# Gate of the feed-forward part applied to the experts' rows and to the shared weights; modulation sums in pairs

## What is computed

```python
c_act = jax.nn.silu(c)
for l in range(DEPTH):                                   # DEPTH = 2
    mod = c_act @ w_mod[l] + b_mod[l]                    # 6 parts of 1024
    sh_m, sc_m, g_m, sh_f, sc_f, g_f = [m[:, None, :] for m in jnp.split(mod, 6, axis=-1)]
    h = rms_norm(x, norm_mix_g[l]) * (1.0 + sc_m) + sh_m
    x = x + g_m * mixer(h, ...)
    h = rms_norm(x, norm_ffn_g[l]) * (1.0 + sc_f) + sh_f
    x = x + g_f * moe_ffn(h, ...)
```

## Time and profile before

| | |
|---|---|
| median of 3 runs | 2122.92 us (2121.61 to 2122.98) |
| the profiled execution | 2122.44 us |
| its span, first to last instruction | 2120.3 us |
| TensorE busy | 2038.6 us |
| VectorE busy | 955.1 us |
| ScalarE busy | 400.2 us |
| GpSimd busy | 59.7 us |
| rate of the transfers while pairs run (page, part 2) | 397 to 412 GB/s in most slices |
| first half of branch 2 ends on TensorE, layer 0 | 197.2 us |
| output projection, layer 0 | 313.5 to 341.1 us |
| shared expert's second product, layer 0 | from 375.4 us |
| pairs of experts, layer 0 | 393.6 to 911.2 us |
| pairs of experts, layer 1 | 1271.7 to 1790.0 us |

### The profile page before, as it was taken

The page is one execution under the profiler, slowest core; times in us unless marked ns, Lnnn a source line. Parts: engine busy times, 40 slices in busy tenths (PEclk is TensorE's granted clock), DMA queues, the critical chain, the costliest instruction groups (busy, mean ns, idle before and its releaser), DMA issues. The chain is left out here.

```text
span 2120.3 us, 30214 instructions
## 1 busy us (share of the span) xinstructions
PE 2038.6 (96%) x11316; PEld 1214.5 (57%) x11316; DVE 955.1 (45%) x1926; ACT 400.2 (19%) x795; POOL 59.7 (3%) x143
## 2 busy tenths in 40 slices
PE   5999999899999999989999989999999997999998
PEld 3847884545445454466588644545545443475475
DVE  3897534333333333359864253433333333252252
ACT  2133211111111111123231011111111112131131
POOL 1000003000000000000000030000000000010000
PEclk9999999999999999999999999999999998998999
DMA  9654548799999999767455548999999997441621
GB/s 348 205 208 164 199 152 342 289 412 401 397 406 400 407 399 400 303 226 231 159 206 192 191 186 336 397 410 398 405 400 404 397 412 240 163 127 28 224 77 43
DMA packets 148133, 598.08 MB, mean 282 GB/s; under 512 B 13036, under 2 KB 17760, under 8 KB 96608
## 3 DMA queue, kind: packets, MB, share of 16 engines
q1 hardware_dynamic: 146656, 594.06, 72.7%
q0 software_dynamic: 1408, 3.10, 0.6%
HBM read 596.07 MB, written 1.05 MB: 282 GB/s over the span
## 5 line engine op out<-in xcount | busy, mean ns | idle before, releaser
L1236 PE MATMUL banks<-weight_ring,h_t 128*64 128x512 f32 x2112 | 464.7, 592 | 3.3 <-DVE h_t L1991 3.3
L1236 PEld LDWEIGHTS banks<-weight_ring,h_t 128*64 128x64 f32 x2112 | 154.8, 137 | 300.8 <-issue 299.0
L1224 PEld LDWEIGHTS banks<-z,sp_ 128*128 128x128 bf16 x3168 | 180.3, 99 | 58.7 <-issue 51.9
L2016 DVE SCALAR_TENSOR_TENSOR o_parts<-banks,slot_weight,o_parts 128x512 fp32r<-128x512 f32 x132 | 99.1, 751 | 245.0 <-ACT o_parts L1522 245.0
L1996 DVE TENSOR_TENSOR z<-banks,z 128x256 f32<-128x256 f32 x66 | 28.0, 425 | 386.5 <-ACT z L1509 386.5
L1224 PE MATMUL banks<-z,sp_ 128*128 128x128 bf16 x3168 | 191.6, 221 | 5.1 <-DVEq L1981 5.1
L930 PE MATMUL banks<-h_t,weight_ring 128*128 128x256 f32 x768 | 170.0, 379 | 0.0
L930 PEld LDWEIGHTS banks<-h_t,weight_ring 128*128 128x128 f32 x768 | 145.4, 190 | 20.0 <-DMA weight_ring<-in_w_in 0.2
L1522 ACT ACTIVATE o_parts<-banks,slot_weight 128x512 fp32r<-128x512 f32 x132 | 90.8, 688 | 278.2 <-PE banks L1261 278.2
L1274 PE MATMUL banks<-o_parts,slot_of 128*128 128x512 f32 x528 | 140.0, 406 | 0.9 <-DVE o_parts L2016 0.9
L2253 PE MATMUL banks<-weight_ring,h_t 128*128 128x512 f32 (+2 forms) x384 | 134.3, 509 | 1.3 <-DMA weight_ring<-in_w_in 1.3
(11 more groups left out here) (479 smaller groups left out, 2139.6 us busy)
## 6 DMA issues: line engine op xcount, KB each, us to landing
weight_ring<-in_w SPq DMA_DIRECT2D x264, 1024.0 KB, 9.8
weight_ring<-in_w_in SPq DMA_DIRECT2D x36, 2048.0 KB, 10.3
slots<-in_w SPq DMA_DIRECT2D x68, 1024.0 KB, 9.1
weight_ring<-in_w_mod SPq DMA_DIRECT2D x24, 2048.0 KB, 11.5
qk<-in_w SPq DMA_DIRECT2D x32, 1024.0 KB, 8.4
...
```

Of the source, the lines that this page charges most:

```text
L1224: mm = nc.tensor.matmul(x_banks[half][:, kk * P:(kk + 1) * P], xn_parts[:, t, c, half * KT // 2 + kk, :], pick_hot[:, i % PAIRS, t, :], st ...
L1236: mm = nc.tensor.matmul(h_bank[own, :], x_blk[:, i, k, own], w13(2 * i + b)[:, :, k, :], start=(k == 0), stop=(k == KT - 1), skip_group_ch ...
L2016: v.scalar_tensor_tensor(o_parts[:, 1, col], o_banks[h][:], own, o_parts[:, 0, col].bitcast(F32), ALU.mult, ALU.subtract).then_inc(o_ready, 1)
```

## The change

**Modulation.** Sums of column chunks are made in pairs: `cols` of chunk c takes the parts of c and c + 1 (the two halves of one part of the modulation) and sums each with 64 columns into its own half of the bank's partitions. VectorE then picks once, with `ident_half`, the sum of the identity's two halves, and `col4` needs no adding of halves. The places change too: in layer 0 the transposes of x now stand ahead of parts 0 to 3 (`first`); sum 6 leaves its place behind the value projections, and pair 6/7 stands between the two halves of the first branch that runs, branch 2 (`half`); pair 8/9 takes the place of sums 7 to 9; sum 12 goes, and pairs 12/13 and 14/15 stand where sums 13 and 14, 15 stood. On ScalarE the copies of parts 0 to 3 go behind the first norm. The row chunks keep their sums.

**Gate.** `gate` of the feed-forward part no longer multiplies the token banks. GpSimd multiplies the shared expert's second weights with it, in place, once they and the gate are there; SyncE loads them behind `wo` 1, no longer as the last of the ring's loads. `o_split` becomes: VectorE writes bank x slot weight x gate to `o_gated`, ScalarE copies that, rounded, to the first part, VectorE subtracts the two for the second. Behind the last pair, `last_add` adds its rows token tile by token tile (before: column half by column half), and VectorE adds the banks to x with one operation each. For that ScalarE copies the last pair's slot matrix once more.

**Rest.** TensorE, not SyncE, frees the eight banks at the start; SyncE issues c ahead of the positions and doesn't wait for GpSimd.

```diff
 MOD_STEPS = {
-    "start": [("part", 0), ("part", 1), ("sum", 0), ("part", 2), ("sum", 1), ("part", 3), ("sum", 2), ("sum", 3)],
-    "ka": [("sum", 4), ("sum", 5)], "va": [("sum", 6)], "aT": [("sum", 7), ("sum", 8), ("sum", 9)],
+    "first": [("part", 0), ("part", 1), ("cols", 0), ("part", 2), ("pad", 0), ("pad", 1), ("pad", 2), ("pad", 3),
+              ("part", 3), ("cols", 2)],
+    "ka": [("sum", 4), ("sum", 5)], "half": [("cols", 6)], "aT": [("cols", 8)],
...
+                            for half in range(2):
+                                own = slice(64 * half, 64 * half + 64)
+                                if c in DVE_CHUNKS:
+
+                                    pe.wait_ge(dve_parts.sem, dve_parts.at(l, c + half - DVE_CHUNKS[0] + 1))
+                                    share = K.ones[:, 0:64]
+                                else:
+
+                                    pe.wait_ge(B[l]["mod_part", c + half].free, B[l]["mod_part", c + half].consumed_at(l))
+                                    share = K.part_share[:].to_broadcast([P, 64])
+                                mm = nc.tensor.matmul(bank[own, :], share, mod_part[c + half], start=True, stop=True,
+                                                      skip_group_check=True)
...
+                pool.wait_ge(shared2_filled.sem, shared2_filled.at(l, 16))
+                pool.wait_ge(gate_ready.sem, gate_ready.at(l))
+                nc.gpsimd.tensor_tensor(slots2[:, 1], slots2[:, 1], broadcast(gate[:, 1, :], 1, 2), ALU.mult)
...
+                def last_add():
+
+                    for t in range(T):
+                        for h in range(2):
+                            if t == 0:
+                                pe.wait_ge(o_ready, nth(last_turn, 2 * second + h))
...
+                        mm.then_inc(y_done.sem, 1)
...
                     for h in range(2):
+                        dve.wait_ge(o_done, nth(it, 2 * i + h))
+                        v.scalar_tensor_tensor(o_gated[h], o_banks[h][:], own, gate[:, 1, h * CHUNK:(h + 1) * CHUNK], ALU.mult,
+                                               ALU.mult).then_inc(o_gated_ready, 1)
+                    for h in range(2):
                         col = slice(h * CHUNK, (h + 1) * CHUNK)
                         dve.wait_ge(o_first_ready, nth(it, 2 * i + h))
-                        v.scalar_tensor_tensor(o_parts[:, 1, col], o_banks[h][:], own, o_parts[:, 0, col].bitcast(F32), ALU.mult,
-                                               ALU.subtract).then_inc(o_ready, 1)
+                        v.tensor_tensor(o_parts[:, 1, col], o_gated[h], o_parts[:, 0, col].bitcast(F32), ALU.subtract)\
+                            .then_inc(o_ready, 1)
...
+                    dve.wait_ge(y_done.sem, y_done.at(l, t + 1))
                     for h in range(2):
                         col = slice(h * CHUNK, (h + 1) * CHUNK)
-                        v.tensor_tensor(y_tmp[:], y_bank[t][h][:], gate[:, 1, col], ALU.mult)\
+                        v.tensor_tensor(K.x[:, t, col], K.x[:, t, col], y_bank[t][h][:], ALU.add)\
                             .then_inc(B[l]["=moe_y", t, h].free, 1)
-                        dve.drain()
-                        v.tensor_tensor(K.x[:, t, col], K.x[:, t, col], y_tmp[:], ALU.add)
-                        dve.drain()
```

134 lines of the change are left out of this document (70 added, 64 removed).

## The result

| | before | after |
|---|---|---|
| median | 2121.29 us (10 runs, 2120.40 to 2124.16) | 2109.14 us (10 runs, 2105.93 to 2117.84) |
| the profiled execution | 2122.44 us, span 2120.3 | 2107.32 us, span 2105.6 |
| mean granted clock of TensorE in it (1.00 is 2.4 GHz) | 0.986 | 0.991 |

The changed kernel takes 0.9941 of the time (95% interval 0.9929 to 0.9953), 12.2 us less. The runs of the changed kernel spread over 12 us, those of before over 4. Each run comes with its mean granted clock, and after the change the two go together: 2105.93 us at 0.993, 2108.20 at 0.990, 2111.45 at 0.987, 2115.50 and 2117.84 at 0.985.

The account below looks back on a forecast made before the run. TensorE, busy for 96% of the span, was taken as the bound. Terms -1.36 - 1.00 - 1.08 - 3.06 - 0.83 = -7.33 us led from 2122.44 to 2115.1 profiled, 2115.5 forecast for the median, range 2111.5 to 2119.5.

Parts of the forecast that it names:

- A pair of sums: Paired column sums: halves run side by side, 1.03 us for a pair against 1.72 for two full sums.
- Between the layers: From layer 0 to layer 1: VectorE's shorter chain of additions lets TensorE start 3.06 us earlier.
- the block's end: From layer 1 to the second block: 0.83 us less, with SyncE's loads last instead of VectorE.
- The sentence of the Trainium skill: Column sums: weight loads overlap a running matmul only where row groups differ, so halves would queue, 1.88 us per pair.
- Part 3: Layer 0 before the experts: sum 12 goes and later sums become pairs, together 1.08 us less.
- The loop's cover: Loop over expert pairs: VectorE's extra step stays hidden, with more than 4 us spare before TensorE needs its result.
- rival 4: Loop over expert pairs: VectorE's two added operations delay TensorE; 0.18 us per pair gives 2127 us; chance 0.07.
- The start's chain: Start of layer 0, behind the last weight chunk: the first projection starts 1.36 us earlier.
- rival 3: Start of layer 0: lower clock lasts longer, last part and pair take 1.7 + 0.9 us more; 2118.1 us; chance 0.10.
- part 2: Inside both layers: moved and paired column sums gain 0.50 us in each layer, 1.00 in both.
- part 5: Loop over expert pairs: VectorE's extra split step costs TensorE 0 for each of the 66 pairs.
- a rival in one place: Between the layers: shorter idle time keeps the clock up, winning up to 2.9 us more; 2112.7 us; chance 0.16.

Follow-up runs that it names:

- experiment 4: Changed kernel with two more VectorE operations, never read, ahead of its additions to x behind the last pair in both layers: 2114.71 us, ratio 0.9960.
- filler: Never-read identity products added in TensorE's waits: kernel before, between the layers only, 2120.99 us; changed kernel, ten waits 2106.97 us, nine waits 2103.24 us.
- the increment back: Changed kernel with the semaphore increment put back on the last product of pair_add, which nobody waits for: 2112.86 us, ratio 0.9948.

## Why the prediction missed

**Right, with the mechanism.** A pair of sums takes 1.01 us (1.03). Sum 6 was worth next to nothing: the next product waits 0.72 us for ScalarE's copy in its place. Between the layers 3.28 us are won (3.06), at the block's end 0.87 (0.83), and SyncE is last there, which experiment 4 shows. The sentence of the Trainium skill (TensorE: Matmul & The Clock Gate, Part 3, "The mechanism") that the prediction set against its 1.03 us does not hold here: both halves use all rows, and the second half's weights are loaded from 196.01 us on, while the first half's product runs from 196.00. The prediction also read it too widely, since the tables of the same part count products that differ only in their columns as running together. Part 3 gave 1.00 up to the first gather (1.08). The loop's cover held: no steady pair became longer, and rival 4 (slower) fell.

**Mis-sized.** The start's chain gave 0.61 of 1.36, since the low clock took the last part and the pair, which was rival 3 at a smaller price; that the row shows 0.97 is the luck of an earlier chunk. Inside layer 0 part 2 gave 0.27 from L1020 to L1121, not 0.50: the first pair costs 1.09 with its change of width, and each product group behind a pair is about 0.1 us longer (L1154 takes 3.72 us, and took 3.61).

**Wrong: part 5, "0 for each of the 66 pairs".** I looked for what could delay TensorE in the loop and took its own products as given. They became 0.017 to 0.027 us shorter for each pair, by the places of tiles: 1.7 us in the first two profiles, which no view of the kernel before could tell. A tolerance for the loop would have covered it, but its size is known only from these runs.

**Wrong: the clock, at 0 in the sum and a rival in one place.** Beside the start I gave it one gap, 2.9 us and 0.16. The profile of before had eight low stretches with 20.9 us of lost work, which a table of windows over the whole span would have shown, and they differ from execution to execution. After the change there are 16.3 and 13.9 us in two profiles of the same kernel. Over the profiles without filler that have before's gap and before's modulation the loss is 20.9 to 24.5, over the five with the whole change 13.9 to 29.4, with 16.3 in the middle. "Fixed" went from 2098.1 to 2099.7 down to 2087.4 to 2092.2. Their middle values, 2099.4 and 2091.6 (two of the five have the slower loop), differ by 7.8 us, those of the first profiles by 10.1; forecast and loop together are 7.3 + 1.7 = 9.0.

**The sum of the miss.** 2115.5 - 2109.14 = 6.4 us. 1.6 are the baseline: ten runs of before have their median at 2121.29, where three had 2122.92 (the later comparisons have 2121.8 to 2122.8, so this term is known to about 1 us). 1.7 are the loop. The other 3 are what is left over, not a measurement. I put them down to the clock, less the 0.6 by which the start and part 2 fell short. The runs' own clocks bear that out in part. Within one kernel a run takes some 1.4 us more for each 0.001 that its mean granted clock is lower (a line through all 159 listed runs, each taken against its kernel's mean). Before has 0.9855 in the mean of 62 runs, the changed kernel 0.989 in 16. By this estimate the clock gives 4 to 5 of the 12.2 us; it is rough, since the mean clock counts waits too. Gate alone has 0.989 (5 runs), modulation alone 0.986 (12), so the higher clock comes with the gate part, whose two gaps became shorter. Whether those gaps are the cause, no run tells. The range, 4 us to each side, had room for one such thing, not for three of one sign.

**Open.** Why the clock falls in the middle of busy stretches is not settled. Eleven of the fourteen profiles have such a fall in the second block (between 1906 and 2096 us, 3.0 to 16.9 us lost); the first two of the changed kernel have none, and that with the increment back has two of 7.7 us. The changed kernel's runs at 0.985, 2115.5 and 2117.8 us, fit such falls; they were not profiled.
